# Alternating two kinds of loads in the opening of a two-layer attention and gMLP trunk

## The reference

```python
a = rms_norm(h, g[0])          # h is x at the start
qkv = a @ w_qkv                # 2048 x (2048 q + 256 k + 256 v)
q = partial_rotary(q, cos, sin); k = partial_rotary(k, cos, sin)
# per kv head: scores over a band of 128 keys, softmax with a sink, times v
o @ w_o
```

## Time and profile before

| | |
|---|---|
| median of 3 runs | 1918.41 us |
| the profiled execution | 1919.33 us, its span 1917.5 us |
| granted clock of TensorE, mean over the span | 0.999 |
| TensorE busy | 1903.7 us of the span (99%) |
| VectorE busy | 1334.8 us (70%) |
| ScalarE busy | 959.4 us (50%) |
| w_hi of whole slabs, mean of one | 1058 ns (676 of them) |
| w_lo of whole slabs, mean of one | 1223 ns (676 of them) |
| one product of 128 x 512, mean busy | 389 to 395 ns, overlapped |
| loads | 370.67 MB, mean 193 GB/s |

### The profile page before, as it was taken

The page is one execution under the profiler, slowest core; times in us unless marked ns, Lnnn a source line. Parts: engine busy times, 40 slices in busy tenths (PEclk is TensorE's granted clock), DMA queues, the critical chain, the costliest instruction groups (busy, mean ns, idle before and its releaser), DMA issues.

```text
span 1917.5 us, 25595 instructions
## 1 busy us (share of the span) xinstructions
PE 1903.7 (99%) x8568; PEld 1567.7 (82%) x8568; DVE 1334.8 (70%) x1846; ACT 959.4 (50%) x1279; POOL 6.6 (0%) x24
## 2 busy tenths in 40 slices
PE   9999999999999999999999999999999999999998
PEld 7777888888888888888888888888888888888886
DVE  7896688647855865686767885787568557846874
ACT  7665475435534543454554454654354445434542
POOL 0000000000000000000000000000000000000000
PEclk9999999999999999999999999999999999999999
DMA  8546476666665665567475656566556665665663
GB/s 312 173 131 215 159 224 190 209 197 182 199 198 176 189 216 188 177 195 231 143 252 176 197 180 216 165 197 219 187 184 189 214 193 185 197 197 173 199 198 110
DMA packets 189438, 370.67 MB, mean 193 GB/s; under 512 B 11728, under 2 KB 11984, under 8 KB 188592
## 3 DMA queue, kind: packets, MB, share of 16 engines
q1 hardware_dynamic: 187760, 362.39, 59.2%
q0 software_dynamic: 1024, 6.69, 1.0%
q10 hardware_dynamic: 576, 0.54, 0.1%
HBM read 367.48 MB, written 2.10 MB: 193 GB/s over the span
## 4 chain that ended last, share of the span: by engine, by line
PE 93%; DVE 3%; DMA 2%; ACT 1%; issue 1%; DVEq 0%; ACTq 0%; SPq 0%
PE acc L412 16%; PE acc L414 16%; PE acc L413 16%; PE scores L412 14%; PE scores L414 14%; PE scores L413 14%; DVE work L1098 1%; DVE w_lo L1067 1%; DMA w_raw<-in_mlp_w_up 1%; DMA w_raw<-in_attn_w_qkv 0%; PE t L434 0%; PE scores L535 0%; PE o L554 0%; PE o L656 0%; PE scores L467 0%
## 5 line engine op out<-in xcount | busy, mean ns | idle before, releaser
L1067 DVE TENSOR_TENSOR w_lo<-w_raw,w_hi 128x1024 fp32r<-128x1024 f32 x676 | 815.7, 1223 | 324.3 <-ACT w_hi L686 307.1
L686 ACT ACTIVATE w_hi<-w_raw 128x1024 fp32r<-128x1024 f32 x676 | 701.1, 1058 | 529.3 <-PE scores L414 208.0
L1098 DVE STREAM_TRANSPOSE work<-s 32x256 f32<-32x256 f32 x544 | 237.1, 436 | 101.1 <-ACT s L851 91.1
L412 PE MATMUL acc<-w_hi,a_hi 128*128 128x512 f32 x768 | 303.5, 395 | 2.3 <-DVE w_lo L1067 2.2
L414 PE MATMUL acc<-w_hi,a_lo 128*128 128x512 f32 x768 | 299.4, 390 | 0.0
L413 PE MATMUL acc<-w_lo,a_hi 128*128 128x512 f32 x768 | 299.1, 389 | 0.0
L412 PE MATMUL scores<-w_hi,a_hi 128*128 128x512 f32 x644 | 250.7, 389 | 0.0
L414 PE MATMUL scores<-w_hi,a_lo 128*128 128x512 f32 x644 | 250.5, 389 | 0.0
L413 PE MATMUL scores<-w_lo,a_hi 128*128 128x512 f32 x644 | 250.5, 389 | 0.0
L412 PE MATMUL acc<-w_hi,b_hi 128*128 128x512 f32 x640 | 249.9, 391 | 0.6 <-DVE b_lo L1114 0.6
L412 PE MATMUL scores<-w_hi,b_hi 128*128 128x512 f32 x640 | 249.2, 389 | 0.0
(11 more groups left out here) (150 smaller groups left out, 1425.4 us busy)
## 6 DMA issues: line engine op xcount, KB each, us to landing
w_raw<-in_mlp_w_up SPq DMA_DIRECT2D x256, 512.0 KB, 3.8
w_raw<-in_mlp_w_down SPq DMA_DIRECT2D x256, 512.0 KB, 4.7
w_raw<-in_sgu_w_in SPq DMA_DIRECT2D x64, 512.0 KB, 4.6
w_raw<-in_attn_w_qkv SPq DMA_DIRECT2D x36, 512.0 KB, 4.6
w_raw<-in_attn_w_o SPq DMA_DIRECT2D x32, 512.0 KB, 4.6
w_raw<-in_sgu_w_out SPq DMA_DIRECT2D x32, 512.0 KB, 4.7
gain<-in_norm_gains POOLq DMA_DIRECT2D x4, 1024.0 KB, 6.7
h<-in_x SPq DMA_DIRECT2D x4, 512.0 KB, 7.1
```

The costliest lines, as they stand in the source:

```text
L412: nc.tensor.matmul(bank[t][:, :], lhsT=act_hi[:, kb, tok], rhs=w1, start=(kb == 0), stop=False)
L686: nc.scalar.activation(w_hi[:, i % SLOTS, :], w_raw[:, i % RAW_SLOTS, :], ACT.Copy).then_inc(hi_made, 1)
L1067: nc.vector.tensor_tensor(w_lo[:, i % SLOTS, :], w_raw[:, i % RAW_SLOTS, :], w_hi[:, i % SLOTS, :].bitcast(F32), ALU.subtract).then_inc(lo ...
L1098: last = nc.vector.transpose(turned[:, :, :, src * 32:src * 32 + 32], part[:, :, :, dst * 32:dst * 32 + 32])
```

## The change

Five edits, all in the opening, with the table of waits that belongs to them.

- SyncE: the loads of the first query block and the quarters of h alternate.
- ScalarE: the rounding of S8 to S12 alternates with the squares; all five come before the read-out of keys and values (S11 and S12 stood behind it).
- VectorE: `w_lo` of S10 moves ahead of the angles, and those of S11 and S12 from behind `r_in` to ahead of it.
- TensorE: the key transposes move from behind (pair 1, tile 1) and (pair 2, tile 0) to behind (pair 2, tile 0) and (pair 2, tile 1).
- VectorE rotates the first tile of queries before it splits S20; and it, not ScalarE, rounds the very first half slab, with a semaphore of its own (`first_hi`).

```diff
             load_block(B_Q, w_qkv[0], 0, slabs=[0])
-            load_h(0)
-            load_block(B_Q, w_qkv[0], 0, slabs=[1])
-            for n in range(1, len(H_PARTS)):
+            for n in range(len(H_PARTS)):
+                load_block(B_Q, w_qkv[0], 0, slabs=[n + 1])
                 load_h(n)
-            load_block(B_Q, w_qkv[0], 0, slabs=range(2, 2 * PAIRS))
+            load_block(B_Q, w_qkv[0], 0, slabs=range(len(H_PARTS) + 1, 2 * PAIRS))
...
-                    pe.wait_ge(part_hi if halved else hi_made, i + 1)
+                    if kb == 0:
+                        pe.wait_ge(first_hi, 1)
+                    elif halved:
+                        pe.wait_ge(part_hi, i)
+                    else:
+                        pe.wait_ge(hi_made, i + 1)
...
-            plain_block(B_Q, a_hi, a_lo, {(1, 1): [lambda: transpose_k(0)], (2, 0): [lambda: transpose_k(1)]})
+            plain_block(B_Q, a_hi, a_lo, {(2, 0): [lambda: transpose_k(0)], (2, 1): [lambda: transpose_k(1)]})
...
-                        if kb // SLAB_KB < HALVED:
+                        if 0 < kb < HALVED * SLAB_KB:
                             split_half(kb)
...
                 split_next(B_KV, 2)
-                square_x(0)
-                split_next(B_KV, 3)
-                for n in range(1, len(H_PARTS)):
+                for n in range(len(H_PARTS)):
+                    split_next(B_KV, 3 + n)
                     square_x(n)
                 take_root()
-                split_next(B_KV, 4)
                 act.wait_ge(norm_done, norms[0])
                 evac(0)
                 evac(1)
-                split_next(B_KV, 5, 6)
...
+                dve.wait_ge(part_landed[0], 16)
+                nc.vector.tensor_copy(w_hi[:, 0, 0:COL], w_raw[:, 0, 0:COL]).then_inc(first_hi, 1)
...
-                split_next(B_KV, 2, 3)
+                split_next(B_KV, 2, 3, 4)
                 rotary_angles()
+                split_next(B_KV, 5, 6)
                 sums[0] += 2 * TOK
...
                 inverse(r_in)
-                split_next(B_KV, 4, 5, 6)
...
-            split_next(B_Q, 6)
...
             rotate_q(B_Q, 0)
+            split_next(B_Q, 6)
             rotate_q(B_Q, 1)
```

More of the change, by code:

```diff
@@ L187, in trunk @@
         x_lo = sem("x_lo")
+        first_hi = sem("first_hi")
         part_hi = sem("part_hi")
@@ L1150, in split_half @@
                     col = slice(k * COL, (k + 1) * COL)
-                    dve.wait_ge(hi_made if k else part_hi, i + 1)
+                    if kb == 0:
+                        dve.wait_ge(first_hi, 1)
+                    elif k == 0:
+                        dve.wait_ge(part_hi, i)
+                    else:
+                        dve.wait_ge(hi_made, i + 1)
                     nc.vector.tensor_tensor(w_lo[:, i, col], w_raw[:, i, col], w_hi[:, i, col].bitcast(F32),
                                             ALU.subtract).then_inc(lo_made if k else part_lo, 1)
+                dve.wait_ge(part_landed[0], 16)
+                nc.vector.tensor_copy(w_hi[:, 0, 0:COL], w_raw[:, 0, 0:COL]).then_inc(first_hi, 1)
                 for kbs in X_PARTS:
```

## The result

The changed kernel takes 1921.11 us, the median of 22 runs, one of which took 6196 us (the other 21: 1919.97 to 1922.30, median 1921.04). The kernel before took 1918.33 us in 22 runs of the same session (1917.60 to 1919.02). The ratio is 1.0014, with an interval of 1.0008 to 1.0020: 2.8 us slower. That is within the 0.2% that the prediction counted as no difference, but outside its range, which ended at 1919.7. The forecast was 1918.6.

The account below looks back on a forecast made before the run. TensorE's waits were taken as the bound, 3.4 us reachable; a stated net of - 0.9 us at S13, + 0.36 for a transpose and two VectorE waits ended + 0.15 at the scores: 1918.6 us, range 1916.7 to 1919.7.

Parts of the forecast that it names:

- The queue of loads: SyncE's loads: nine 512 KB transfers of 1.44 us between S8 and S13; S13 lands at 35.1, h3 at 33.7.
- The net of + 0.15 us: First scores: TensorE waits half a microsecond for VectorE's copies and starts at 57.55 against 57.42 before.
- The chain behind h3: ScalarE and VectorE, last square through read-outs, sines, key rotation and `w_lo`: TensorE starts S13 at 41.85, waiting 2.4 us.
- The terms of my sum ahead of S13: TensorE: S10 and S11 waits - 2.17, S13 wait + 2.4, start - 0.54 + 0.3; stated net - 0.9 us.
- the transpose still to do: TensorE: one key transpose, moved behind the start of S13, adds 0.36 us there.
- The end of the query block: VectorE rotates first queries from 52.15, not waiting for S20's `w_lo`; TensorE transposes at 53.25 instead of 53.63, 0.4 us gained.
- The clock: Rival, TensorE behind S13's wait: half rate loses 2 us, scores 58.2, time 1919.2; chance 0.14 together with a later h3.
- the forecast's 57.55 for the scores: First scores: VectorE's rotations and copies, 5.3 us from 52.15, let TensorE start at 57.55.
- The first half slab: Opening: VectorE's copy, taken as 0.6 us, starts real products 0.1 to 0.4 us before 5.43; gain not kept.
- The chance of a later h3: Part of the clock rival: wait before S13 over 3 us, time up to 1920.5; chance 0.14 together with the clock.

Follow-up runs that it names:

- the experiment that held the clock: Changed kernel with twelve unused products added on TensorE ahead of its wait for S13: 1921.35 us, ratio 1.0016.

## Why the prediction was wrong

- **The queue of loads: the step that failed.** "The same nine stand between them after the change, in another order, and the pipe is never empty there, so S13 still lands at about 35.1." I counted transfers and not when each may be issued. The pause of 1.6 us ahead of S9 was filled by h0; with S9 first it was not, and the rate fell to 281 GB/s and then to 200 to 227 (why it fell that second time is open, see below). S13 landed at about 36.3 and not 35.1, and h3 was squared at 35.06 and not 33.7. With the queue kept full the same place gives 33.72 (h3 alone moved), and one load put back in the changed kernel gives 34.28 and takes 1.8 us off. Exchanging the loads within each turn takes off 3.1, but moves h3 up a place as well. The net of + 0.15 us that I had worked out for a landing at 33.7 came out at + 1.3 and + 1.0 in these two kernels, with h3 at or near it; the interval of each holds + 0.15 too.
- **The chain behind h3: right.** Its five links sum to 8.1 us in the forecast (33.7 to 41.8) and 8.1 in the trace (35.06 to 43.2). The wait stands at S13, 2.96 us for 2.4. TensorE was through with S12 at 40.3 and not 39.5; 0.33 us of that is the later start of the query block (27.61 against 27.28). The trace of before could have told the rest: TensorE's 15.5 us from 27.28 to 42.77, less its waits and one transpose, are 13.0 and not the 12.2 of nine slab steps (12.7 in the changed kernel, 27.61 to 40.3). The terms of my sum ahead of S13 (- 2.17, + 2.4, - 0.54, + 0.3) add up to 0.0 and not to the - 0.9 that I wrote, which is the difference of the two positions of S13; these 0.7 us and the transpose still to do make up most of it. Neither slip moves the forecast, since h3 sets when S13 can start.
- **The end of the query block: right in form.** The first query rotation started at 53.64, 1.5 us behind the forecast's 52.15; S13 was 1.4 late. Putting the rotation ahead of S20 does what I said.
- **The clock: the rival's place, a small price.** It fell from 43.9 to 47.3. The forecast's 57.55 for the scores became 59.54: 1.49 of the 1.99 us is the later first rotation, and 0.50 lies behind it. There the second read-out waited 2.03 us for TensorE's products and VectorE 0.56 for that read-out; in the kernel with one load moved back, where the clock stayed up, first rotation to scores took 5.23 us (53.21 to 58.44) and here 5.90 (53.64 to 59.54). The chain of waits of the changed kernel agrees, for it runs from S13 on through TensorE's products and not through S20's load, up to that read-out (start, us, what):

```profile
43.26 0.50 PE acc L412
...
55.37 0.24 PE acc L414
55.64 0.70 ACT s L818
```

TensorE was the later of two branches, but not by much: `w_lo` of S20, which stands on VectorE ahead of the second rotation, ended at 55.8 (54.59 and 1.22), and so that rotation could have started 0.5 us ahead of 56.36 at best. So I read the fall's own price as 0.5 to 0.7 us. That is worked out from two traces; the experiment that held the clock did not show it as a gain, and the pair of kernels with h0 moved back shows 0.3. Nor does the length of the wait alone say whether the clock falls: 2.57 us were followed by the lower level, 2.80 (with the added products) were not.
- **The first half slab: no effect, as said.** The copy took 0.43 us, where I had taken 0.6 and set the estimate of 0.43 from the Trainium skill ("VectorE: DVE Perf Modes", on the two-port 2x mode) beside it; the estimate from the page was the right one. The first real product came 0.14 us earlier (5.29 for 5.43); in the other kernels with this edit it started between 5.05 and 5.70. What starts later, at 27.61, shows that even this was not kept.
- **The chance of a later h3.** The rival had "a longer wait, over 3 us because h3 comes late", at up to 1920.5. The late h3 is what happened (the wait stayed just under 3), and I gave it too little, and too low an end: the range should have followed from pricing one missed turn in the queue (1.3 us) on top.

Left open: why the rings ran at 200 to 227 GB/s from 24 to 27 us although, by the issues, S10, h1, S11 and h2 were all under way by 25.4. `sink_rows` has a part in this stretch (with it moved the rate recovered at 25), but not in h3's landing; `pos_i`, issued just ahead of it, was not moved. In the kernel before the packets of both small loads were moved from 24 to 28 us too, at 378 to 408 GB/s, so they alone don't lower the rate. Also open is the remaining 0.6 to 0.7 us between the scores' delay (2.1 to 2.2 us) and the medians' difference (2.8), which single executions can't show.

## What to carry to other kernels

When loads are reordered, write down for each not its place in the queue but what must happen before it can be issued: a load that waits for nothing is worth most in the pause ahead of one that waits, and moving it behind that one can leave the queue short. Then follow the last transfer that a serial chain hangs on, since waits taken away at its front come back in one piece at its end. Of a wait that replaces two, ask whether it is long enough to bring the clock down, but price that by what the engines beside TensorE leave uncovered, which here was 0.3 to 0.7 us by the traces.

## What the runs showed of the hardware

- A wait of TensorE of 2.31 us left the granted clock at 1.00; waits of 2.57, 2.96, 3.39 and 3.74 us were followed by 0.50, for 3.4 us in the changed kernel. But one of 2.80, in the kernel with added products, left it at 1.00, so their length alone does not say which of them bring the clock down. One execution each.
- Issuing h2 took SyncE 1.69 us, where the other issues took 0.37 to 0.74; it happened at 23.71, with four loads under way. In the other two kernels with this order of loads and the small load in place the same issue took 1.93 and 2.05 us, with the small load moved 0.47.
- Loads of 512 KB went on at a rate below 230 GB/s for 3 us while several were under way, where the kernel before moved 381 to 408 in the same microseconds.
- The landing of S20 moved between executions without an edit near it: 4.8 us after issue in the kernel before, 6.55 us in the one with added products.
